# Nineteen picks of two windows summed beside TensorE: scaled by ScalarE, added by GpSimd, taken in by one identity product

## What is computed

```python
def block(args):
    xblk, idb, gb = args                     # 128 tokens, their 128 expert numbers, their gates
    u_sel = jnp.take(u, idb, axis=0)
    h = jax.nn.gelu(jnp.einsum('td,ted->te', xblk, u_sel), approximate=False)
    v_sel = jnp.take(v, idb, axis=0)
    return jnp.einsum('te,ted->td', gb * h, v_sel)
```

## Time and profile before

| | us |
|---|---|
| median of 3 runs | 2708.25 (2706.5 to 2708.64) |
| the profiled execution | 2708.39 |
| its span | 2706.6 |
| mean granted clock of TensorE | 0.981 of full |
| PE busy | 2513.9 (93%) |
| DVE busy | 1761.8 (65%) |
| ACT busy | 996.6 (37%) |
| POOL busy | 666.8 (25%) |
| DMA, whole span | mean 292 GB/s |

### The profile page before, as it was taken

How to read it: one execution, slowest core, us unless ns; L and a number is a source line. 1 busy time by engine, 2 the same in 40 slices (tenths; PEclk the granted TensorE clock), 3 DMA queues, 4 the chain that set the end, 5 groups by cost and what they waited for, 6 DMA issues and landing times.

```text
span 2706.6 us, 29540 instructions
## 1 busy us (share of the span) xinstructions
PE 2513.9 (93%) x10053; PEld 1584.0 (59%) x10053; DVE 1761.8 (65%) x3962; ACT 996.6 (37%) x2038; POOL 666.8 (25%) x636
## 2 busy tenths in 40 slices
PE   8989998899998999988987899999999999999999
PEld 4544444365544665443432357885788668865787
DVE  2678876656767667768777576654665556637654
ACT  1236322234323364223222245433544444424543
POOL 0144443333554334434444120001000110002000
PEclk9999999899999999989999999999999999999999
DMA  7699999999999999999999724543254405523452
GB/s 299 253 410 416 418 416 421 413 422 421 397 421 421 421 409 386 422 419 421 421 421 420 314 115 171 186 164 132 100 196 143 185 32 217 186 107 123 162 193 95
DMA packets 111488, 791.03 MB, mean 292 GB/s; under 512 B 12995, under 2 KB 15702, under 8 KB 20358
## 3 DMA queue, kind: packets, MB, share of 16 engines
q0 software_dynamic: 74464, 540.07, 48.5%
q1 hardware_dynamic: 36902, 249.44, 24.3%
HBM read 788.39 MB, written 4.22 MB: 293 GB/s over the span
## 4 chain that ended last, share of the span: by engine, by line
PE 65%; DMA 17%; DVE 12%; ACT 3%; issue 2%; POOL 1%; SPq 0%; DVEq 0%; ACTq 0%; POOLq 0%
PE psum L1520 16%; PE psum L1637 13%; PE psum L1199 10%; DMA arena<-in_peer_uv,scratch 9%; PE psum L1594 8%; DMA weights<-in_peer_uv,scratch 7%; PE psum L1596 4%; DVE arena L2482 2%; DVE weights L2482 2%; PE psum L1305 2%; PE psum L1313 1%; PE psum L1176 1%; PE psum L1291 1%; PE psum L1398 1%; PE psum L1280 1%
## 5 line engine op out<-in xcount | busy, mean ns | idle before, releaser
L1520 PE MATMUL psum<-weights,scratch 128*128 128x512 f32 x1024 | 487.2, 624 | 76.8 <-ACT scratch L1975 76.4
L1520 PE MATMUL psum<-arena,scratch 128*128 128x512 f32 x1024 | 477.6, 612 | 56.3 <-ACT scratch L1975 55.9
L2855 DVE TENSOR_TENSOR piece<-weights,piece 128x2048 fp32r<-128x2048 f32 x128 | 292.1, 2292 | 181.7 <-ACT piece L2068 181.7
L2482 DVE SCALAR_TENSOR_TENSOR arena<-arena,x 128x1024 f32<-128x1024 f32 x256 | 310.3, 1224 | 152.9 <-DMA arena<-in_peer_uv,scratch 151.2
L3009 POOL DMA_INDIRECT weights<-in_peer_uv,scratch x256 | 290.1, 1133 | 451.5 <-PE psum L1520 399.4
L2482 DVE SCALAR_TENSOR_TENSOR weights<-weights,x 128x1024 f32<-128x1024 f32 x256 | 310.1, 1226 | 138.6 <-DMA weights<-in_peer_uv,scratch 135.7
L3009 POOL DMA_INDIRECT arena<-in_peer_uv,scratch x256 | 294.2, 1149 | 390.0 <-PE psum L1520 374.0
L1520 PEld LDWEIGHTS psum<-weights,scratch 128*128 128x128 f32 x1024 | 196.6, 199 | 324.2 <-issue 226.6
L1520 PEld LDWEIGHTS psum<-arena,scratch 128*128 128x128 f32 x1024 | 193.2, 195 | 298.8 <-issue 203.6
L1969 ACT ACTIVATE scratch<-scratch 128x2 f32<-128x2 f32 x255 | 51.9, 203 | 845.3 <-DVE arena L2482 426.9
L1637 PE MATMUL psum<-piece,hidden 128*128 128x512 f32 x1536 | 358.9, 390 | 0.0
(11 more groups left out here) (284 smaller groups left out, 2832.5 us busy)
## 6 DMA issues: line engine op xcount, KB each, us to landing
weights<-in_w_up SPq DMA_DIRECT2D x64, 1024.0 KB, 4.8
weights<-in_w_down SPq DMA_DIRECT2D x64, 1024.0 KB, 4.8
weights<-in_w_kv_b SPq DMA_DIRECT2D x16, 1024.0 KB, 9.4
weights<-in_a_w_in SPq DMA_DIRECT2D x5, 2048.0 KB, 12.3
weights<-in_peer_w_q SPq DMA_DIRECT2D x8, 1024.0 KB, 9.2
weights<-in_w_q_b SPq DMA_DIRECT2D x8, 1024.0 KB, 9.4
weights<-in_a_w_out SPq DMA_DIRECT2D x4, 2048.0 KB, 8.4
weights<-in_w_qkv_a SPq DMA_DIRECT2D x3, 2048.0 KB, 16.6
```

Of the source, the lines that this page charges most:

```text
L1520: mm = pe.matmul(psum[g.bank][:, :], diagonal[:, n % DIAGONALS, :], row[:, D + half * BANK:D + (half + 1) * BANK], start=(k == 0), stop=(k ...
L2482: dve.scalar_tensor_tensor(u, u, 1.0, x[:, n // SEL % NT, :], ALU.mult, ALU.mult, accum_out=dots[:, n % SEL:n % SEL + 1]).then_inc(dotted. ...
L2855: dve.tensor_tensor(split_piece[n][1][:, :], raw_piece[n], split_piece[n][0][:, :], ALU.subtract)\
```

## The change

Two tables name pairs: eight in window 1, eleven in window 2. Of each such pair the second pick is no longer mixed by PE. ACT, in place of the diagonal, scales the `v` half by the weights, in the buffer itself (`scale_pick`); the first such pick of a window is written straight into `added`, 1024 columns of `heads_arena`. POOL, at the point where it would wait for PE to release that pick's buffer, waits for the scaling, adds the buffer to `added` (`add_pick`), waits for its own addition, and issues the gather. At pair 48 PE adds `added` to the two banks by two matmuls with the identity. The diagonals are numbered by themselves (`diagonal_of`), and every wait on `value_mixed` counts by tables. The core of the diff:

```diff
+BESIDE_PAIRS = {1: (10, 13, 24, 29, 34, 37, 39, 41), 2: (10, 13, 15, 20, 24, 27, 29, 31, 34, 37, 39)}
+BESIDE_FLUSH = 48
...
+        added = heads_arena[:, 0:D]
...
+        pick_scaled = sem("pick_scaled")
+        pick_added = sem("pick_added")
...
+        added_count, sum_count, mixed_count, flush_count, diagonal_picks = {}, {}, {}, {}, []
+        mixes = 0
+        for n in range(WINDOWS * SEL):
+            w, (pair, second_of_pair) = n // SEL, divmod(n % SEL, 2)
+            if second_of_pair and pair in BESIDE_PAIRS.get(w, ()):
+                added_count[n] = len(added_count) + 1
+                if pair != BESIDE_PAIRS[w][0]:
+                    sum_count[n] = len(sum_count) + 1
+            else:
+                mixes += 1
+                mixed_count[n] = mixes
+                diagonal_picks.append(n)
+            if second_of_pair and w in BESIDE_PAIRS and pair == BESIDE_FLUSH:
+                mixes += 1
+                flush_count[w] = mixes
+        diagonal_of = {n: d for d, n in enumerate(diagonal_picks)}
...
-            slot_release[slot] = (value_mixed.sem, picks[-1] + 1)
+            slot_release[slot] = (value_mixed.sem, mixed_count[picks[-1]])
...
-                    sp.wait_ge(value_mixed.sem, WINDOWS * SEL)
+                    sp.wait_ge(value_mixed.sem, mixes)
...
                         bank_free(g)
                 for k in (2 * pair, 2 * pair + 1):
                     n = w * SEL + k
+                    if n in added_count:
+                        continue
                     row = gathered[n % GATHER_SLOTS]
-                    pe.wait_ge(diagonal_ready.sem, n + 1)
+                    pe.wait_ge(diagonal_ready.sem, diagonal_of[n] + 1)
                     for half, g in enumerate(mixed[w]):
-                        mm = pe.matmul(psum[g.bank][:, :], diagonal[:, n % DIAGONALS, :], row[:, D + half * BANK:D + (half + 1) * BANK],
+                        mm = pe.matmul(psum[g.bank][:, :], diagonal[:, diagonal_of[n] % DIAGONALS, :], row[:, D + half * BANK:D + (half + 1) * BANK],
                                        start=(k == 0), stop=(k == SEL - 1))
+                    mm.then_inc(value_mixed.sem, 1)
+                if w in BESIDE_PAIRS and pair == BESIDE_FLUSH:
+                    pe.wait_ge(pick_added, sum_count[w * SEL + 2 * BESIDE_PAIRS[w][-1] + 1])
+                    for half, g in enumerate(mixed[w]):
+                        mm = pe.matmul(psum[g.bank][:, :], identity, added[:, half * BANK:(half + 1) * BANK], start=False, stop=False)
                     mm.then_inc(value_mixed.sem, 1)
...
             def make_diagonal(n):
-                k = n % SEL
-                if n >= DIAGONALS:
-                    act.wait_ge(value_mixed.sem, n - DIAGONALS + 1)
-                act.activation(diagonal[:, n % DIAGONALS, :], identity, ACT.Copy, scale=weight[:, k:k + 1])\
+                k, d = n % SEL, diagonal_of[n]
+                if d >= DIAGONALS:
+                    act.wait_ge(value_mixed.sem, mixed_count[diagonal_picks[d - DIAGONALS]])
+                act.activation(diagonal[:, d % DIAGONALS, :], identity, ACT.Copy, scale=weight[:, k:k + 1])\
                     .then_inc(diagonal_ready.sem, 1)
+
+            def scale_pick(n):
+
+                k, v = n % SEL, gathered[n % GATHER_SLOTS][:, D:2 * D]
+                first = n not in sum_count
+                if first and n // SEL - 1 in flush_count:
+                    act.wait_ge(value_mixed.sem, flush_count[n // SEL - 1])
+                act.activation(added if first else v, v, ACT.Copy, scale=weight[:, k:k + 1]).then_inc(pick_scaled, 1)
 
             def diagonals(i):
                 act.wait_ge(weights_ready.sem, i + 1)
                 make_diagonal(2 * i)
-                make_diagonal(2 * i + 1)
+                if 2 * i + 1 in mixed_count:
+                    make_diagonal(2 * i + 1)
+                else:
+                    scale_pick(2 * i + 1)
...
-                dve.wait_ge(value_mixed.sem, (w + 1) * SEL)
+                dve.wait_ge(value_mixed.sem, mixed_count[(w + 1) * SEL - 1])
...
         def _(pool):
+            def add_pick(n):
+
+                pool.wait_ge(pick_scaled, added_count[n])
+                if n in sum_count:
+                    if sum_count[n] > 1:
+                        pool.wait_ge(pick_added, sum_count[n] - 1)
+                    pool.tensor_tensor(added, added, gathered[n % GATHER_SLOTS][:, D:2 * D], ALU.add).then_inc(pick_added, 1)
+                    pool.wait_ge(pick_added, sum_count[n])
+
             def gathers(w):
 
                 rows = A["peer_uv"].rearrange("l e d -> (l e) d")
...
                     n, h = w * SEL + k, k // TOPK
                     if k % TOPK == 0:
                         pool.wait_ge(routed.sem, w * PEER_HEADS + h + 1)
-                    if n >= GATHER_SLOTS:
-                        pool.wait_ge(value_mixed.sem, n - GATHER_SLOTS + 1)
+                    if n - GATHER_SLOTS in added_count:
+                        add_pick(n - GATHER_SLOTS)
+                    elif n >= GATHER_SLOTS:
+                        pool.wait_ge(value_mixed.sem, mixed_count[n - GATHER_SLOTS])
```

## The result

| | before | changed |
|---|---|---|
| median of 14 runs each | 2708.63 us | 2713.15 us |
| lowest to highest | 2706.41 to 2710.38 | 2709.55 to 2716.36 |
| profiled execution (span) | 2708.39 (2706.6) | 2710.1 (2708.3) |

The ratio is 1.0017, with a 95% interval of 1.0009 to 1.0024: about 4.5 us slower, where 7.6 us less were forecast. The loss is clear of zero, but it is smaller than the 0.2% (5.4 us) that the prediction drew as its line between "the same" and "slower". The profiled execution of the changed kernel lies near the fast end of its runs, 1.7 us above the one of before, so its trace shows less than half of the loss.

What follows compares the result with a forecast made beforehand. The DMA gather stream was taken as the bound, except where it sags because PE is late. Terms: 6.4 (window 2) + 1.7 (window 1) - 0.5 (DVE held) = 7.6 us; 2708.4 - 7.6 = 2700.8 us, range 2696.5 to 2714.

Steps and rivals of the forecast that it cites:

- GpSimd against DVE: -0.5 us: Adds hold DVE products 0.6 us each; only one add, in window 1 near 670 us, costs time: 0.5 us (0 to 2.35).
- The waits move: Rival, 0.22: with PE lighter, DVE held by adds or a late GpSimd makes the same sags; about 2708 us.
- the prediction's own sign of being wrong: The prediction is wrong if DMA sags stand although PE is idle in them; then DVE or GpSimd makes them.
- DVE becomes the bound: Rival, 0.08: full 2.35 us holds make DVE pairs 0.95 us too long; 17 adds lose 16 us, 2724.6 us.
- PE, removed: 8.1 us: Taking 19 picks off PE closes DMA sags: 6.4 us back in window 2, 1.7 us in window 1.
- GpSimd, added: 2.35 us, cost 0: 17 adds of 2.35 us (1.27 to 3.43) before gathers in windows 1 and 2 cost nothing; PE's relief brings gathers forward.
- ScalarE: 1.055 us, cost 0: 19 scalings of 1.055 us replace diagonals of 0.394 us; PE's backlog of two pairs covers the 12.6 us more.
- Flush, free: Two flushes of 1.72 us put back on PE at pair 48, where PE has idle time; the wait for the sum is void.
- The early picks, nothing: Picks of pairs 10, 13 and 15 in window 2 come off where DMA keeps its full rate, so they return nothing.
- GpSimd's code: 0: Code loading before the first add, pair 17 of window 1, takes 0 to 22.2 us; taken as covered, zero.
- that rival: Code loading stops the gathers, 0.10: GpSimd loads up to 22.2 us at pair 17 of window 1; at the top 2716.9 us.
- the cover I gave it: Queued transfers near 560 us cover a GpSimd stop of 8.5 us, less 2.35 for the add: 6.1 us.

Runs made afterwards that it cites:

- the three profiles compared above: Profiles of the kernel before, the changed kernel, and the changed kernel without GpSimd's additions (sums of 17 picks left out; 2704.76 against 2708.15 us).

## Why the prediction was wrong

The forecast (-7.6 us) and the result (+4.5 us) lie 12.1 us apart. By the medians 7.4 of them are the price of the additions (8 us in place of 0.5, the first step below), and 4.7 are relief that did not come (3.4 in place of 8.1, the second).

*GpSimd against DVE: -0.5 us.* This is the step that failed. I scaled the small row by the columns to 0.6 us for each add and charged one place only. Measured, DVE loses 1.75 us for each add, and all of them together cost 8 us in the medians. The Trainium skill (SBUF — State Buffer, § Who interferes with whom) says that the one which issues second is blocked until the first has finished. On the length of the hold the trace agrees: a product of 1.22 us took 3.90 beside an add of 2.35. On the order it agrees only in part: of the 17 held DVE operations 10 began after the add, and 7 began up to 0.65 us before it and were held all the same. I had that rule and the upper bound of 2.35 us, and took a value near the lower end from adds of 128x128 that last 0.45 us, too short to show more. And I held the total against DVE's 43 free us of 150. Free time on average does not take up a stop of 2.35 us: between a product and the gather it lets go lie the weights, ScalarE's diagonals and PE's mix, and all of them start late.

Two rivals of the prediction had this mechanism. "The waits move" (0.22) said that DVE, held by adds, makes the same sags, at about 2708 us. This is what the profile shows from 1040 to 1080 us, where the sag stands although PE is idle, the prediction's own sign of being wrong; its time is 5 us short. "DVE becomes the bound" (0.08) had the full hold, with 16 us, twice the price measured.

*PE, removed: 8.1 us.* Its places were right (7.5 us of relief where I looked for 8.1, though shared 2.5 and 5.0 rather than 1.7 and 6.4; that the sum comes so near is partly luck); its worth was not. I took a sag that closes for time that is won. Later stretches gave 4.0 us of it back, and by the medians 2.1 to 3.6 us are kept. With 41 picks off it is no more, so what is left there is not taken away by relieving PE. What sets this floor stays open. Moving the flush, shortening the scalings and keeping the granted clock up gained nothing. The DMA is full until after the last gather's issue in the three profiles compared above; the shortfall behind window 2 lies between 1101 and 1511 us, and what makes it was not tried.

*GpSimd, added: 2.35 us, cost 0.* The adds took 2.344 to 2.582 us, median 2.35. Filling in their place for about as long costs 2 us by the medians, and part of that may be DVE's held casts.

*ScalarE: 1.055 us, cost 0.* A scaling took 1.133 us; shortening it changed nothing that can be measured. *Flush, free*: it goes with a sag of 2.0 us, and moving it gave back nothing that can be measured. *The early picks, nothing*: so it was.

*GpSimd's code: 0.* The first add began at 556.08 us, 0.10 us after the end of the gather's issue, and took 2.35 us. There is no stop, and that rival is gone. It did not need the cover I gave it: the 5.95 us of the Trainium skill (GPSIMD Engine Reference, § Instruction dispatch) are not seen here.

## What to carry to other kernels

Here an operation that reads SBUF on GpSimd took its length from VectorE too, at each of its 17 places. Price such an operation at its whole length on VectorE's chain, and compare that with doing it on VectorE, which here was shorter (1.28 against 1.75 us, and at a place of one's own choice). A sag in the throughput of the bound resource is an upper limit on what a relief returns: leave the relieved work out in one run before building its replacement, since that run costs little and says what there is to win.

## What was not expected of the hardware

- A product whose record has begun can still be overtaken: the one at 1059.14 us began 0.47 us before the add and ended 1.08 us after it, nearly the 1.22 us that it needs alone. A gather issue alone does not hold a product: in the kernel before over 150 products begin while an issue runs, and the longest of all 512 took 1.30 us. Six of the seven operations that were overtaken had begun while an issue ran in front of the add, the seventh as it ended. Whether that is why they were overtaken, no run tests.
- The reverse does happen: in the kernel before, of the gather issues that begin inside a product, half take 1.5 us or more, up to 1.99, where one alone takes 0.94.
- A 128x2 operation of 0.16 us is held as long as a product is: 1.95 us in the run with additions alone, up to 3.03 in the changed kernel. Over the changed kernel these 255 operations lose 12.1 us, nearly as much as the 512 products (15.2).
- Cutting an addition in four makes it 60% longer (3.8 us for four quarters against 2.38). Four undisturbed quarters of 0.72 us would make 2.9; the other 0.9 us come with quarters that took up to 1.79 us.
